# Queries of eight decode samples computed as rows, one weight place fewer and one key place more, sigmoids of the gates put off

## The chip, the cores and the metric

The kernel runs on one core of a Trainium2 chip. The metric is the time of one execution on the device, in microseconds (us). The core has a matmul engine (PE, with its weight loads shown apart as PEld), VectorE (DVE), ScalarE (ACT), GpSimd (POOL), and a queue (SP) that here only issues DMAs; 16 DMA engines move data between HBM and on-chip memory.

## The reference

One decoder layer serves a prompt of 256 tokens and 8 samples of one token each, with the same weights (float32).

```python
h = rms_norm(x, g_norm1) * (1.0 + sc1) + sh1
proj = h @ w_in
q, k, v, glu_a, glu_b, gate_a, gate_c = jnp.split(proj, ...)
q = rms_norm(q.reshape(B, S, N_HEADS, HEAD_DIM), g_q)      # 8 heads x 64
k = rms_norm(k.reshape(B, S, N_HEADS, HEAD_DIM), g_k)
attn = moba_attention(q, k_all, v_all, pos0, alibi_slopes()) @ w_attn_proj
u = glu_a * jax.nn.sigmoid(glu_b)
cv = depthwise_causal_conv(conv_in, w_dwconv) + b_dwconv    # 31 taps, 512 channels
cv = jax.nn.silu(layer_norm(cv, g_conv_ln, b_conv_ln)) @ w_conv_proj
mix = (jax.nn.sigmoid(gate_a) * attn + jax.nn.sigmoid(gate_c) * cv) @ w_out
x = x + gt1 * mix
h2 = rms_norm(x, g_norm2) * (1.0 + sc2) + sh2
x = x + gt2 * ((jax.nn.silu(f_g) * f_u) @ w_ffn_out)
```

`sh1`, `sc1`, `gt1` and the rest come from `silu(c) @ w_ada + b_ada`, with a `c` for the prompt and for each sample. In `moba_attention` every query of a sample scores 2,048 cached positions (16 pages of 128), ranks the 8 blocks of 256 by the mean score, and keeps the best three and its own position. The cached keys and values are found by a page table: 4.2 MB of keys and as much of values for each sample.

## The kernel before

The program has a stream of instructions for each engine, written by hand in the order in which they run; semaphores tie them together. Activations lie transposed: 1,024 channels as 8 tiles of 128 partitions, and 264 columns, 256 of the prompt and 8 of the samples. `fp32r` products are made from split operands: a weight tile and an activation each become a high part (ACT copies it, rounded) and a low part (the rest after subtraction), and three matmuls (high by low, low by high, high by high) add up in one bank.

**Before the loop.** PE runs tiles q0 to q3, k0 to k3, v0 to v3, a0 and b0 of `w_in`. q0 goes unsplit (`tile`, L1452, float32). Each of the others (`split`, L1465 to L1467, 24 matmuls) needs the high part of its weights from ACT (`high`, tensor `phi`, a ring of four) and the low part (`rest`, tensor `wrest`, which lies over the weights themselves). POOL makes the low parts (L589), DVE that of q2 (L1027). ACT takes each finished tile out of its bank (`raw`), squares q and k for the head norm, and PE sums the squares (`head_sums`, L1496). `spread_norm` (L1510) spreads the inverse roots, and `head_norm` on DVE (L1046) applies them.

The samples' queries are the last 8 columns of tiles q0 to q3. Once q3 is out, ACT squares them, PE sums them (L1523), ACT takes the root, DVE normalises (L1032), PE turns them into rows in 12 small matmuls (L1527, L1528) amid tile k0, ACT and DVE split them (`qsplit`), and `spread_query` (L1482) copies the query of one sample to all partitions, amid tile k1.

**Scores.** `multiply` (L1057) and `add_up` (L1064) on DVE take a quarter of one sample's keys: 4 of 16 pages, 128 x 2,048 elements each. A sample has four such quarters ("halves" by the parameter's name). Keys come by gathers that POOL issues (`gather_k`, 2.1 MB, half of a sample), into three places: two in `kring`, the third in place 2 of the weight ring `wring`. A gather waits until the chunk three before it is multiplied. Four quarters and the multiply of a fifth run before the loop.

**The loop over b = 0 to 7.** Iteration b finishes the choice of blocks and the softmax of sample b, weighs the values of sample b-1 (`weigh_values`, L1604, 16 matmuls of 512 columns that the profile counts as 32), does head b of the prompt's attention, a part of the convolution (20 taps for b < 6: ACT multiplies, POOL adds, L578), and two or three tiles of the gates (`g0` to `g15`), which ACT passes through a sigmoid as it takes them out of their bank. DVE meanwhile scores sample b+1, in four slots between its small operations. The weights of the gate tiles are `mix0` to `mix6`, loaded alternately into places 0 and 1; the third tile of a `mix` (`THIRD`) is finished in the next iteration, and only then may SP issue the load that takes its place.

**After the loop.** UNITS: 8 tiles of the convolution's projection (`cp`), 8 of attention's (`ap`), 8 of the output (`o`), 44 of the FFN's first and 8 of its second matmul. For each, ACT makes the high part (`whi`) and DVE the low part (`wlo`, L1129), in a ring of four.

**Weights.** SP issues all weight loads in the order of SLOTS, each when the former load of its place is used up. PLACE says which place: before, q, k, v and glu go to places 1, 2, 0 and 1.

## Time and profile before

| | |
|---|---|
| median of 3 runs | 591.69 us (584.13, 591.69, 594.33) |
| the profiled execution | 585.78 us, its span 584.0 us |
| granted TensorE clock, mean | 0.958 |
| PE busy | 523.6 us (90%) |
| DVE busy | 394.2 us (67%) |
| ACT busy | 292.1 us (50%), of it 46.2 us loads of activation tables |
| POOL busy | 170.0 us (29%) |
| DMA | 159.31 MB, 273 GB/s over the span |

Times below count from the start of the span. By the timeline the program has four stretches: up to 39 us the first loads and the modulation; 39 to 106 us the tiles q to b0; 106 to 300 us the loop; then the units up to 584 us. A busy share is an average over these; what bounds a stretch is read from it.

### The profile page before, as it was taken

Reading aid. Unit: us, or ns where it says so; the run is one execution under the profiler, and the core shown is the slowest. Engines: PE = TensorE matmul, PEld = TensorE weight load, DVE = VectorE, ACT = ScalarE, POOL = GpSimd, SP = SyncE. Lnnn points to the kernel's source line nnn. Section 1 sums busy time; section 2 is a strip of 40 time slices with the busy share of each in tenths; the row PEclk is TensorE's granted clock in tenths of the full one; section 3 lists DMA queues with packets and bytes.
Section 4 is the critical chain, followed back from the end, with each engine's and each line's share of the span. In section 5 each row is a group of like instructions: output and inputs, shape, how many; then the busy total and the mean of one; then the engine's idle time right before and its main releaser. Section 6 shows DMA issues by size and latency. Waiting matters only on the chain.

```text
span 584.0 us, 10410 instructions
## 1 busy us (share of the span) xinstructions
PE 523.6 (90%) x4180; PEld 441.1 (76%) x4180; DVE 394.2 (67%) x602; ACT 292.1 (50%) x519; POOL 170.0 (29%) x232
## 2 busy tenths in 40 slices
PE   3769899988979879798798999899999999999997
PEld 3658678865655646556458888799999999999996
DVE  1742674789999998999765865567565656554441
ACT  3144433587777877655653532293444444434331
POOL 8326377287778776750100000000000000000000
PEclk9589898897999999999979999999999999999999
DMA  8999459698999999999676989946466446476501
GB/s 306 370 369 388 165 189 346 224 357 296 405 399 397 420 401 416 366 366 414 260 296 245 387 291 374 364 148 213 150 221 206 147 158 164 122 192 169 153 20 38
DMA packets 82128, 159.31 MB, mean 273 GB/s; under 512 B 2573, under 2 KB 61113, under 8 KB 76952
## 3 DMA queue, kind: packets, MB, share of 16 engines
q1 hardware_dynamic: 76256, 89.27, 45.8%
q0 software_dynamic: 5120, 67.71, 28.9%
q10 hardware_dynamic: 703, 1.67, 0.8%
q8 instruction: 33, 0.54, 0.4%
q14 instruction: 16, 0.12, 0.1%
HBM read 156.39 MB, written 2.72 MB: 272 GB/s over the span
## 4 chain that ended last, share of the span: by engine, by line
PE 57%; DVE 21%; DMA 10%; issue 5%; ACT 4%; POOL 1%; SPq 1%; ACTq 1%; DVEq 0%; POOLq 0%
PE acc L1580 12%; PE acc L1581 12%; PE acc L1582 12%; DVE prod L1057 7%; DMA wring<-in_w_in 6%; DVE sall L1064 4%; PE acc L1452 3%; DMA wring<-in_w_ffn_in 2%; PE acc L1465 2%; PE acc L1467 2%; PE acc L1466 2%; DMA pr<-in_page_table 2%; PE acc L1384 2%; PE chain L1604 2%; ACT L623 1%
## 5 line engine op out<-in xcount | busy, mean ns | idle before, releaser
L1129 DVE TENSOR_TENSOR wlo<-wring,whi 128x1024 fp32r<-128x1024 f32 (+2 forms) x84 | 92.0, 1097 | 72.2 <-ACT whi L623 71.4
L623 ACT ACTIVATE whi<-wring 128x1024 fp32r<-128x1024 f32 (+2 forms) x84 | 80.1, 958 | 83.2 <-PE acc L1582 77.4
L1580 PE MATMUL acc<-xlo,whi 128*128 128x264 f32 x384 | 110.2, 287 | 3.5 <-DVE wlo L1129 1.3
L1581 PE MATMUL acc<-xhi,wlo 128*128 128x264 f32 x384 | 108.8, 283 | 0.0
L1582 PE MATMUL acc<-xhi,whi 128*128 128x264 f32 x384 | 108.8, 283 | 0.0
L578 POOL TENSOR_TENSOR cvT<-cvT,cprod 128x256 f32<-128x256 f32 x120 | 87.9, 732 | 42.4 <-ACT cprod L623 27.6
L1452 PE MATMUL acc<-hT,wring 128*128 128x264 f32 x336 | 92.1, 418 | 3.7 <-DMA wring<-in_w_in 3.3
L1580 PEld LDWEIGHTS acc<-xlo,whi 128*128 128x128 f32 x384 | 72.3, 188 | 5.8 <-issue 3.1
L1452 PEld LDWEIGHTS acc<-hT,wring 128*128 128x128 f32 x336 | 63.3, 200 | 17.6 <-DMA wring<-in_w_in 3.7
L1064 DVE TENSOR_REDUCE sall<-prod 128x32 f32<-128x2048 f32 x32 | 73.0, 2281 | 0.4
L1581 PEld LDWEIGHTS acc<-xhi,wlo 128*128 128x128 f32 x384 | 72.4, 188 | 0.1
L1582 PEld LDWEIGHTS acc<-xhi,whi 128*128 128x128 f32 x384 | 72.0, 187 | 0.0
L623 ACT ACTIVATE cprod<-u,vt 128x256 f32<-128x256 f32 x120 | 53.6, 500 | 13.7 <-POOL cvT L578 12.5
L1581 PE MATMUL acc<-fhi,wlo 128*128 128x264 f32 x208 | 59.2, 284 | 0.0
L1582 PE MATMUL acc<-fhi,whi 128*128 128x264 f32 x208 | 58.9, 283 | 0.0
L1057 DVE TENSOR_TENSOR prod<-kring,qbc 128x2048 f32<-128x2048 f32 x22 | 50.0, 2273 | 1.3 <-PE qbc L1482 0.7
L1580 PE MATMUL acc<-flo,whi 128*128 128x264 f32 x176 | 50.0, 284 | 0.3 <-ACT yn L623 0.3
L623 ACT ACT_TABLE_LOAD x36 | 46.2, 1283 | 2.3 <-PEq L1772 1.7
L589 POOL TENSOR_TENSOR wrest<-wring,phi 128x1024 fp32r<-128x1024 f32 x14 | 33.9, 2428 | 39.4 <-ACT phi L623 39.3
L1582 PEld LDWEIGHTS acc<-fhi,whi 128*128 128x128 f32 x208 | 39.1, 188 | 0.0
L1581 PEld LDWEIGHTS acc<-fhi,wlo 128*128 128x128 f32 x208 | 39.1, 188 | 0.0
L1465 PE MATMUL acc<-hsplit,phi 128*128 128x264 f32 x120 | 37.7, 314 | 0.8 <-POOL wrest L589 0.8
...
## 6 DMA issues: line engine op xcount, KB each, us to landing
...
```

Of the source, the lines that this page charges most:

```text
L578: g.tensor_tensor(cvT[:, t, 0:S], cvT[:, t, 0:S], cprod[:, i % CONV_RING, :], ALU.add)\
L589: g.tensor_tensor(low, w, high.bitcast(F32), ALU.subtract).then_inc(rest_by_pool, 1)
L623: return nc.scalar.activation(out, in_, f, **kw)
L1057: v.tensor_tensor(prod[:, :, :], k_place[chunk % K_RING][:, g:g + n, :], qbc[b % 2][:, :].unsqueeze(1).to_broadcast([P, n, A]), ALU.mult). ...
L1064: v.tensor_reduce(sall[:, b % 2, n * half:n * half + n, :].rearrange("p g h -> p (g h)"), prod[:, :, :].rearrange("p g (h d) -> p (g h) d" ...
L1129: v.tensor_tensor(wlo[:, place, 0:n, :], w, whi[:, place, 0:n, :].bitcast(F32), ALU.subtract)\
L1384: ins = mm(bank[32 * t:32 * t + 32, 0:P], cT[:, kk, :], w[:, kk, P * t:P * t + P], start=kk == 0, stop=kk == KD - 1)
L1452: ins = mm(bank[:, 0:R], w[:, k, P * t:P * t + P], src[:, k, :], start=k == 0, stop=k == KD - 1)
L1465: mm(bank[:, 0:R], high[:, k, :], hlo[:, k, :], start=k == 0, stop=False)
L1580: mm(bank[:, 0:R], whi[:, place, k - k0, :], lo[:, k, :], start=k == 0, stop=False)
L1581: mm(bank[:, 0:R], wlo[:, place, k - k0, :], hi[:, k, :], start=False, stop=False)
L1582: ins = mm(bank[:, 0:R], whi[:, place, k - k0, :], hi[:, k, :], start=False, stop=k == nk - 1)
```

## The change

1. **Queries as rows.** When the weights of q are there, 8 matmuls multiply the samples' 8 columns of `hT` by all 512 columns of q, in four row groups of one bank (`chain`, zeroed earlier by a DVE memset that moves here from the end of the head norms). ACT copies the bank, and one matmul adds the four groups up into rows 0 to 7 and 32 to 39 of `psS`. ACT squares them, DVE reduces, ACT takes the root, DVE multiplies by the gain and the inverse root, and ACT and DVE split them. `spread_query(0)` stands amid tile q1, `spread_query(1)` after k0. The old way (one sum, 12 turning matmuls, their copies) is gone.
2. **Places.** Place 2 of the ring holds only `ada2` before the keys; q, k, v, glu go to places 1, 0, 1, 0, and the `mix` loads start with place 1. So k waits for `ada3`, v for q, and glu for k.
3. **Scores earlier.** Six quarters run before the loop, and slot s of iteration b does quarter 4b+6+s instead of 4b+4+s. Slots 2 and 3 of iteration 6 are empty.
4. **Gathers.** Another order between the `rest` operations, below. `rest("q2")` moves from DVE to POOL.
5. **Gates.** ACT copies the gate tiles in the loop and applies the sigmoid later in four operations over four tiles (1,056 columns) each: around the last `values`, and at units 3 and 7.
6. **Smaller.** The head norms use three banks instead of four, in two groups of three around v3 and a0; PE waits for the probabilities of sample b-1 ahead of the block sums of b; the third tile ends before the mask matmuls.

```diff
-PLACE = dict(zip(SLOTS, [0, 1, 2, 0, 1, 2, 0, 1] + [n % 2 for n in range(B - 1)]))
-PLACE.update(conv=2, attn=1, mod4=0, mod5=0, out0=3, mod6=2, out1=4, mod7=0, mod8=2, mod9=0, mod10=3, mod11=4)
+PLACE = dict(zip(SLOTS, [0, 1, 2, 0, 1, 0, 1, 0] + [(n + 1) % 2 for n in range(B - 1)]))
+PLACE.update(conv=2, attn=0, mod4=1, mod5=1, out0=3, mod6=2, out1=4, mod7=1, mod8=2, mod9=1, mod10=3, mod11=4)
...
+            pool.dma_start(grow, g_q.rearrange("(o d) -> o d", o=1).to_broadcast([32 + B, DH])).then_inc(grow_in, 16)
...
-            for name in ON_POOL:
+            pool.wait_ge(w_full[PLACE["q"]], 32 * LOADS["q"])
+            gather_k(0)
+            pool.wait_ge(qpart_ready, 1)
+            for _, _, name in SPLITS:
                 rest(name)
-                if name == "q1":
-                    gather_k(0)
-                if name == "k0":
+                if name == "q3":
                     gather_k(1)
+                if name == "k2":
+                    pool.wait_ge(ada_used, 3)
+                    gather_k(2)
                 if name == "v0":
-                    pool.wait_ge(acc_full, NUMBER[LAST_FILL["k"]] + 1)
-                    gather_k(2)
-                if name == "v2":
                     gather_k(3)
-                if name == "v3":
+                if name == "a0":
+                    gather_k(4)
+                if name == "b0":
                     gather_v(0, 0)
                 if name == "b1":
-                    gather_k(4)
+                    gather_k(5)
...
-                gather_k(CH * b + 5)
+                gather_k(CH * b + 6)
                 add_taps(b, 2)
-                gather_k(CH * b + 6)
+                gather_k(CH * b + 7)
...
-            for t in range(KD):
+            def input_high(t):
                 act.wait_ge(h_ready, min(t + 1, H_BY_DVE))
                 if t >= H_BY_DVE:
                     act.wait_ge(h_by_act, t - H_BY_DVE + 1)
                 func(hhi[:, t, :], hT[:, t, :], ACT.Copy).then_inc(hhi_ready, 1)
+            input_high(0)
+            input_high(1)
+            act.wait_ge(consts, 3)
+            act.wait_ge(qpart_ready, 1)
+            func(pvm[:, :], chain[:, :], ACT.Copy).then_inc(qpart_copied, 1)
+            for t in range(2, 5):
+                input_high(t)
+            act.wait_ge(qrow_ready, 1)
+            func(qsq, psS[both, :], ACT.Square).then_inc(qsq_ready, 1)
+            for t in range(5, KD):
+                input_high(t)
+            act.wait_ge(qss_ready, 1)
+            func(qroot, qss, ACT.Sqrt, scale=1.0 / DH, bias=eps[both, :]).then_inc(qroot_ready, 1)
             high("q2")
+            act.wait_ge(qfull_ready, 1)
+            func(qsplit[both, :], qfull, ACT.Copy).then_inc(qs_ready, 1)
             raw("q", 0)
             high("q3")
+            func(snat, qfull[0:B, :].rearrange("p (a n) -> p a n", a=2), ACT.Copy).then_inc(qs_ready, 1)
...
             raw("q", 3)
...
             square("q", 3)
+            high("k2")
             raw("k", 0)
...
-                freed(func(gates[:, n, :], bank[:, 0:R], ACT.Sigmoid), f"g{n}")
+                freed(func(gates[:, n, :], bank[:, 0:R], ACT.Copy), f"g{n}")
+            def open_gates(first):
+                for n in range(first, first + 4):
+                    wait_freed(act, f"g{n}")
+                func(gates[:, first:first + 4, :], gates[:, first:first + 4, :], ACT.Sigmoid).then_inc(gates_open, 1)
...
+            open_gates(8)
             values(B - 1)
+            open_gates(12)
...
+                if n_unit in (3, 7):
+                    open_gates(n_unit - 3)
...
+            v.memset(chain[:, :], 0.0).then_inc(chain_zero, 1)
...
-            for t in range(KD):
+            def input_low(t):
                 dve.wait_ge(hhi_ready, t + 1)
                 v.tensor_tensor(hlo[:, t, :], hT[:, t, :], hhi[:, t, :].bitcast(F32), ALU.subtract).then_inc(hlo_ready, 1)
-            rest("q2")
+            by_head = "p (h d) -> p h d"
+            for t in range(3):
+                input_low(t)
+            dve.wait_ge(qsq_ready, 1)
+            v.tensor_reduce(qss, qsq.rearrange(by_head, d=DH), AX.X, ALU.add).then_inc(qss_ready, 1)
+            at_gain = mark(v.tensor_tensor(qgain.rearrange(by_head, d=DH), psS[both, :].rearrange(by_head, d=DH),
+                                           grow.unsqueeze(1).to_broadcast([32 + B, H, DH]), ALU.mult))
+            input_low(3)
             dve.wait_ge(qroot_ready, 1)
-            step(v.reciprocal(qroot, qroot))
-            v.scalar_tensor_tensor(qsn, qT[:, :, S:R], vec[:, V_GQ:V_GQ + 1], qroot, ALU.mult, ALU.mult).then_inc(qsn_ready, 1)
+            at_root = mark(v.reciprocal(qroot, qroot))
+            dve.wait_ge(dve_step, at_root)
+            v.tensor_tensor(qfull.rearrange(by_head, d=DH), qgain.rearrange(by_head, d=DH),
+                            qroot.unsqueeze(2).to_broadcast([32 + B, H, DH]), ALU.mult).then_inc(qfull_ready, 1)
+            for t in range(4, 6):
+                input_low(t)
             dve.wait_ge(qs_ready, 1)
-            v.tensor_tensor(qsplit[32:32 + B, :], psS[32:32 + B, :], qsplit[32:32 + B, :].bitcast(F32),
+            dve.wait_ge(qfull_ready, 1)
+            v.tensor_tensor(qsplit[32:32 + B, :], qfull[32:32 + B, :], qsplit[32:32 + B, :].bitcast(F32),
                             ALU.subtract).then_inc(qlo_ready, 1)
+            for t in range(6, KD):
+                input_low(t)
...
-            score(0, 0)
-            score(0, 1)
-            score(0, 2)
+            for half in range(STEPS):
+                score(0, half)
+            score(1, 0)
             dve.wait_ge(head_root, 1)
             v.reciprocal(headsums, headsums).then_inc(head_inv, 1)
-            score(0, 3)
-            for n in range(4):
-                head_norm(n)
-            dve.wait_ge(norm_read, 4)
-            v.memset(chain[:, :], 0.0).then_inc(chain_zero, 1)
-            multiply(1, 0)
-            for n in range(4, 6):
+            score(1, 1)
+            for n in range(6):
                 head_norm(n)
...
+                def multiply_next(slot):
+                    to, half = divmod(STEPS * b + 6 + slot, STEPS)
+                    if to < B:
+                        multiply(to, half)
...
-                if b >= 1:
-                    multiply_next(0)
+                multiply_next(0)
...
+                dve.wait_ge(gates_open, 3 + t // 4)
...
-            tile("q0", w, 0, hT)
-            split("q1")
+            pe.wait_ge(chain_zero, 1)
+            pe.wait_ge(gs1_ready, 2)
+            for k in range(KD):
+                rows = slice(32 * (k % 4), 32 * (k % 4) + B)
+                ins = mm(chain[rows, :], hT[:, k, S:R], w[:, k, :], start=k < 4, stop=k >= 4)
+            ins.then_inc(qpart_ready, 1)
+            tile("q0", w, 0, hT, k1=2)
+            pe.wait_ge(consts, 3)
+            pe.wait_ge(qpart_copied, 1)
+            mm(psS[both, :], rowsel, pvm[:, :], start=True, stop=True).then_inc(qrow_ready, 1)
+            tile("q0", w, 0, hT, k0=2)
+            split("q1", k1=4)
+            pe.wait_ge(qs_ready, 1)
+            pe.wait_ge(qlo_ready, 1)
+            spread_query(0)
+            split("q1", k0=4)
             split("q2")
             head_sums(0)
             split("q3")
             head_sums(1)
-            split("k0", k1=2)
-            pe.wait_ge(qsq_ready, 1)
-            mm(chain[:, 0:32], halves[:, :], qsq.rearrange("p t b -> p (t b)"), start=True, stop=True).then_inc(qsq_summed, 1)
-            split("k0", k0=2, k1=6)
-            pe.wait_ge(qsn_ready, 1)
-            for t in range(4):
-                nc.tensor.transpose(psS[0:B, P * t:P * t + P], qsn[:, t, :], ident[:, :])
-                ins = mm(psS[32:32 + B, P * t:P * t + P], qsn[:, t, :], ident[:, :], start=True, stop=True)
-            ins.then_inc(qs_turned, 1)
-            split("k0", k0=6)
-            split("k1", k1=3)
-            pe.wait_ge(qs_ready, 2)
-            pe.wait_ge(qlo_ready, 1)
-            spread_query(0)
-            split("k1", k0=3)
+            split("k0")
+            spread_query(1)
             head_sums(2)
+            split("k1")
             head_sums(3)
             split("k2")
             head_sums(4)
             head_sums(6)
             split("v0", k0=4)
             head_sums(7)
-            spread_query(1)
             split("v1")
             split("v2")
-            split("v3", k1=4)
-            for n in range(4):
+            for n in range(3):
                 spread_norm(n)
-            split("v3", k0=4)
-            for n in range(4, 6):
+            split("v3")
+            split("a0")
+            for n in range(3, 6):
                 spread_norm(n)
-            split("a0")
             split("b0")
...
+                if b >= 1:
+                    pe.wait_ge(p_ready, b)
...
+                if b - 1 in THIRD:
+                    tile(THIRD[b - 1], mix, 2, hT, k0=4, k1=6)
                 if b >= 1:
                     turn_values(b - 1)
                 else:
                     split("a1")
-
                 if b - 1 in THIRD:
-                    tile(THIRD[b - 1], mix, 2, hT, k0=4, k1=7)
+                    tile(THIRD[b - 1], mix, 2, hT, k0=6)
...
-                if b - 1 in THIRD:
-                    tile(THIRD[b - 1], mix, 2, hT, k0=7)
```

**On PE, the start of the q tiles** (`acc` is the bank of tile q0, then of q1; `chain` and `psS` are the banks of the queries). Before:

```order
66 L1441 MATMUL acc<-ident,prod 128x128 [waits rows_by_dve] x2
67 L1452 MATMUL acc<-hT,wring 128x264 [waits h_ready,acc_free1,w_full1]
68 L1452 MATMUL acc<-hT,wring 128x264 [waits h_ready] x4
69 L1452 MATMUL acc<-hT,wring 128x264 [waits h_by_act] x3
70 L1465 MATMUL acc<-hsplit,phi 128x264 [waits hlo_ready,acc_free0,rest_by_pool]
```

Now:

```order
66 L1479 MATMUL acc<-ident,prod 128x128 [waits rows_by_dve] x2
67 L1553 MATMUL chain<-wring,hT 8x512 [waits gs1_ready,chain_zero,w_full1]
68 L1553 MATMUL chain<-wring,hT 8x512 x7
69 L1490 MATMUL acc<-hT,wring 128x264 [waits h_ready,acc_free1]
70 L1490 MATMUL acc<-hT,wring 128x264 [waits h_ready]
71 L1558 MATMUL psS<-pvm,pg 40x512 [waits qpart_copied,consts]
72 L1490 MATMUL acc<-hT,wring 128x264 [waits h_ready] x3
73 L1490 MATMUL acc<-hT,wring 128x264 [waits h_by_act] x3
74 L1502 MATMUL acc<-hsplit,phi 128x264 [waits hlo_ready,acc_free0,rest_by_pool]
```

Nine matmuls of 512 columns stand ahead of and amid q0; the rows from L1523 to L1528 amid k0 are gone.

**On DVE, iteration 6 of the loop** (`prod` and `sall` are the multiply and the sum of a quarter; `u`, `cvT` the layer norm of the convolution). Before:

```order
262 L1218 TENSOR_TENSOR s<-s,small 128x136 [waits mb_ready]
263 L1064 TENSOR_REDUCE sall<-prod 128x32 [waits k_used]
264 L1224 TENSOR_REDUCE tiny<-s 128x8 [waits e_ready]
265 L1113 TENSOR_SCALAR cprod<-acc 128x264 [waits acc_full]
266 L1115 TENSOR_TENSOR cvT<-cvT,cprod 128x1056 [waits acc_free0]
267 L1117 TENSOR_TENSOR u<-cvT 128x4x264 [waits dve_step]
268 L1057 TENSOR_TENSOR prod<-kring,qbc 128x2048 [waits scored,k_full0]
269 L1231 TENSOR_TENSOR tiny<-small,s 128x8 [waits tot_ready]
270 L1233 RECIPROCAL tiny<-tiny 128x8 [waits dve_step]
```

Now:

```order
269 L1255 TENSOR_TENSOR s<-s,small 128x136 [waits mb_ready]
270 L1261 TENSOR_REDUCE tiny<-s 128x8 [waits e_ready]
271 L1148 TENSOR_SCALAR cprod<-acc 128x264 [waits acc_full]
272 L1150 TENSOR_TENSOR cvT<-cvT,cprod 128x1056 [waits acc_free0]
273 L1152 TENSOR_TENSOR u<-cvT 128x4x264 [waits dve_step]
274 L1268 TENSOR_TENSOR tiny<-small,s 128x8 [waits tot_ready]
275 L1270 RECIPROCAL tiny<-tiny 128x8 [waits dve_step]
```

Slots 2 and 3 are empty, so two multiplies and two sums are gone from between the small operations; the small operations stand as before.

**On POOL, between the low parts of the weights** (`wrest`). Before:

```order
52 L589 TENSOR_TENSOR wrest<-wring,phi 128x8x128 [waits w_full0,phi_ready,acc_full,rows_ready]
53 L553 DMA kring<-in_cache_k,rowof 128x4096
54 L589 TENSOR_TENSOR wrest<-wring,phi 128x8x128 [waits phi_ready] x2
55 L553 DMA kring<-in_cache_k,rowof 128x4096
56 L589 TENSOR_TENSOR wrest<-wring,phi 128x8x128 [waits phi_ready] x4
57 L553 DMA wring<-in_cache_k,rowof 128x4096 [waits acc_full]
58 L589 TENSOR_TENSOR wrest<-wring,phi 128x8x128 [waits phi_ready] x2
59 L553 DMA kring<-in_cache_k,rowof 128x4096 [waits k_used]
60 L589 TENSOR_TENSOR wrest<-wring,phi 128x8x128 [waits phi_ready]
61 L553 DMA vring<-in_cache_v,rowof 128x4096
```

Now:

```order
56 L561 DMA kring<-in_cache_k,rowof 128x4096 [waits w_full0,w_full1,acc_full,rows_ready]
57 L597 TENSOR_TENSOR wrest<-wring,phi 128x8x128 [waits phi_ready,qpart_ready]
58 L597 TENSOR_TENSOR wrest<-wring,phi 128x8x128 [waits phi_ready] x2
59 L561 DMA kring<-in_cache_k,rowof 128x4096
60 L597 TENSOR_TENSOR wrest<-wring,phi 128x8x128 [waits phi_ready] x3
61 L561 DMA wring<-in_cache_k,rowof 128x4096 [waits ada_used]
62 L597 TENSOR_TENSOR wrest<-wring,phi 128x8x128 [waits phi_ready] x2
63 L561 DMA kring<-in_cache_k,rowof 128x4096 [waits k_used]
64 L597 TENSOR_TENSOR wrest<-wring,phi 128x8x128 [waits phi_ready] x4
65 L561 DMA kring<-in_cache_k,rowof 128x4096 [waits k_used]
66 L597 TENSOR_TENSOR wrest<-wring,phi 128x8x128 [waits phi_ready]
67 L561 DMA vring<-in_cache_v,rowof 128x4096
```

The first gather stands ahead of the first low part, which waits for the queries' matmuls; six chunks of keys instead of five are gathered ahead of the loop's taps (the last ones are not among these rows), and the first values come behind the low part of b0, which needs the gated unit's weights.

## Rows read from the trace of the kernel before

**Rows 1.** windows: us, length; busy us of PE, PEld, DVE, ACT, POOL; clock, DMA share, GB/s.

```profile
39.00:44.30 5.30, 5.17 (x17) 4.09 (x17) 4.38 (x8) 4.94 (x12) 3.44 (x2) 0.68 1.05 387
44.30:47.30 3.00, 3.00 (x26) 2.97 (x25) 2.55 (x6) 1.65 (x3) 1.18 (x1) 1.00 1.06 391
63.00:67.00 4.00, 3.96 (x18) 3.23 (x19) 3.36 (x2) 1.00 (x4) 0.99 (x1) 0.64 0.61 192
152.70:177.00 24.30, 20.70 (x117) 13.41 (x116) 23.89 (x32) 18.35 (x39) 18.36 (x25) 1.00 1.03 397
252.00:283.00 31.00, 26.78 (x147) 18.28 (x145) 29.98 (x42) 17.66 (x32) 6.73 (x9) 1.00 0.94 374
```

**Rows 2.** timeline of PE: start, us, instruction, idle before and its releaser.

```profile
39.13 5.51 PE L1452 MATMUL acc<-hT,wring 128*128 128x264 f32 x16 [2.32 <-DMA wring<-in_w_in]
57.11 0.27 PE L1527 MATMUL psS<-ident,pg 128*8 128x128 f32 x1
59.18 0.40 PE L1465 MATMUL acc<-hsplit,phi 128*128 128x264 f32 x1
63.04 0.46 PE L1482 MATMUL qbc<-qsplit,qsel 40*128 40x512 f32 x1 [1.76 <-DVE qsplit L1034]
```

**Rows 3.** timeline of DVE before the loop and at its start.

```profile
40.83 4.89 DVE L1021 TENSOR_TENSOR hsplit<-hT,hsplit 128x264 fp32r<-128x264 f32 x8 [0.92 <-ACT hsplit L623]
62.21 0.68 DVE L1034 TENSOR_TENSOR qsplit<-psS,qsplit 8x512 fp32r<-8x512 f32 x1 [5.47 <-ACT qsplit L623]
63.60 2.29 DVE L1057 TENSOR_TENSOR prod<-kring,qbc 128x2048 f32<-128x2048 f32 x1 [0.71 <-PE qbc L1482]
105.97 0.16 DVE L1160 COPY gsT<-small 128x4 f32<-128x4 f32 x1 [9.40 <-PE small L1618]
```

**Rows 4.** page, costliest groups: busy us, mean ns, idle before.

```profile
L623 ACT ACT_TABLE_LOAD x36 | 46.2, 1283 | 2.3 <-PEq L1772 1.7
L589 POOL TENSOR_TENSOR wrest<-wring,phi 128x1024 fp32r<-128x1024 f32 x14 | 33.9, 2428 | 39.4 <-ACT phi L623 39.3
```

**Rows 5.** chain that ended last: start, us, what.

```profile
30.04 9.05 DMA wring<-in_w_in
...
128.95 2.29 DVE sall L1064
149.06 1.28 ACT L623
150.36 0.32 ACT s L623
...
191.09 26.40 DMA wring<-in_w_in
217.54 3.71 PE acc L1452 x8
223.99 1.28 ACT L623
229.84 2.30 DVE sall L1064
```

**Rows 6.** timeline of DVE, the sums that end two iterations.

```profile
154.93 2.29 DVE L1064 TENSOR_REDUCE sall<-prod 128x32 f32<-128x2048 f32 x1
179.41 2.29 DVE L1064 TENSOR_REDUCE sall<-prod 128x32 f32<-128x2048 f32 x1
```

**Rows 7.** timeline of PE, iteration 6 of the loop.

```profile
256.90 3.62 PE L1604 MATMUL chain<-vring,pg 128*8 128x512 f32 x32
282.71 0.39 PE L1618 MATMUL small<-quad,sall 128*128 128x4 f32 x2 [0.81 <-DVE sall L1064]
```

**Rows 8.** timeline of ACT around the last values.

```profile
295.45 2.10 ACT L623 ACTIVATE cvT<-cvT,vt 128x264 f32<-128x264 f32 x4
301.61 0.60 ACT L623 ACTIVATE pvm<-chain 128x512 f32<-128x512 f32 x1 [2.40 <-PE chain L1604]
```

**Rows 9.** timeline of DVE, low parts of attention's rows.

```profile
315.67 1.46 DVE L1268 TENSOR_TENSOR fhi<-oT,fhi 128x264 fp32r<-128x264 f32 x4 [0.49 <-ACT fhi L623]
```

74 lines of the change are left out of this document (31 added, 43 removed).

## The prediction

> **What bounds the kernel now.** I read the windows first: the busy time of each engine by stretch says which engine can end it. In an ordinary iteration of the loop DVE is busy 23.89 of 24.30 us, PE 20.70, and the DMA engines move 397 GB/s at a share of 1.03 [rows 1]. So DVE sets the pace and the DMA has next to nothing to spare; a saving on PE, ACT or POOL is worth only what DVE's idle time holds. Iteration 6 is the exception: PE 26.78 and DVE 29.98 of 31 us. Before the loop it is PE: DVE stands idle 9.40 us until PE's first block sums at 105.97 [rows 3]. The FFN at the end is PE's alone, and the change leaves it as it is. The timelines then show what lies in PE's way before the loop, and the chain of waits which waits in the loop count.
>
> **Queries as rows (before the loop, PE's path).** Out go the 12 turning matmuls, 57.11 to 59.18: 2.1 us [rows 2]; the wait for the split queries, 1.76 us [rows 2]; and perhaps the slow stretch behind that wait. In 63 to 67 us the granted clock is 0.64 [rows 1]; between the levels 2.4 and 1.2 GHz that is 2.9 us at the low one, or 1.4 us lost. Together 5.3 us. In come eight matmuls of 512 columns in four row groups. The nearest row is `weigh_values`, 16 such in 3.62 us [rows 7], so 1.8 us, and at most 3.6 at the low clock. The adding matmul uses the whole array and gets no such overlap: four times 3.62/16 is 0.9 us, 1.8 at the low clock. The stretch from 39 to 44.3 has clock 0.68 [rows 1], so I take 3.0 for both (bounds 2.7 and 5.4).
>
> Then the wait at the new `spread_query(0)`. Behind the adding matmul come in turn: ACT 0.6 [rows 8], four DVE operations of 512 columns at 0.68 [rows 3], a small reciprocal, taken as 0.35, ACT 0.6, and three low parts of `hT` that stand between, 4.89/8 = 0.61 each [rows 3]: 6.1 us. PE has six matmuls of q0 (5.51/8 = 0.69 each [rows 2], 4.1) and half of q1 (12 of 26 in 3.00 us [rows 1], 1.4) to cover it. It waits 0.6 us, and a little more for the last two low parts. I take 0.7, with bounds 0 and 4. In 3.7, out 5.3: **-1.6 us**. The bounds of the parts give -2.6 to +4.1, and up to +5.5 if the slow stretch stays all the same.
>
> **All low parts on POOL** cost POOL one more of 2.43 us [rows 4]. In the old trace POOL waits 39.3 us for ACT's high parts [rows 4], so it is ACT's order that paces it: 0. Without this cover each low part costs PE up to 2.4.
>
> **Zeroing `chain`** moves 0.4 us or so of DVE work (the price of 512 columns lies under the 0.68 of a two-input operation [rows 3]) ahead of the tiles of x. The chain then runs through the q load, 30.04 to 39.09 [rows 5], so it can cost all of it or nothing: **+0.4**.
>
> **Six quarters before the loop.** The scores can start about 13 us earlier than 63.60 [rows 3], near 50.5. The two added operations and a half, 3 x 2.28, lie in DVE's 9.40 us of idle time. The first slot's multiply now also stands ahead of iteration 0's block sums, so iteration 0 has the same DVE work behind them as before, and 1 to 5 have four full slots as before: 24.48 us from one end to the next [rows 6]. The work saved is all in iteration 6. There PE runs on from DVE's scores and waits only 0.81 us for the last sum [rows 7]; its order (two gate tiles, two sums over the convolution, the prompt's scores) does not change, and the small chain on DVE does not wait for the quarters. So of 9.1 us that leave DVE, **-0.8** arrive.
>
> **Sigmoids put off.** The program now holds 16 table loads instead of 36: 20 x 1.28 us [rows 4] leave ACT. What counts is where the chain runs through one: at 149.06 and at 223.99 [rows 5], 1.28 us each. The first lies in iteration 1, from 128.95 [rows 5] to 154.93 [rows 6], 26.0 us, which is 1.5 more than 24.48: **-1.5**. The second lies in the stretch from 179.41 [rows 6] to 229.84 [rows 5], two iterations in 50.4 instead of 49.0. In the same stretch PE waited for a load of gate weights that took 26.40 us, and then ran eight matmuls in 3.71 us instead of about 2 [rows 5]. That load is issued when the third tile is done, which now is before the mask matmuls, 1 to 2 us earlier, and it was about 1 us late. Both causes go: **-1.4**. Iteration 0 keeps its sigmoid of the gated unit and its table loads: 0.
>
> What comes back: four sigmoids of 1,056 columns. Four of 264 take 2.10 us [rows 8], the upper price of one; half is the lower. The first has 2.40 idle us of ACT before it [rows 8] for itself and a table load of 1.28, so it may end a little late; the others stand between high parts that are made three units ahead. **+0.5**, bounds 0 and 4.
>
> On the loads, the row shows 1.28 us, and the operation behind starts at once (149.06 and 1.28 is 150.34, and the exponential starts at 150.36 [rows 5]). The Trainium skill, "ScalarE: Activation LUTs", section "What ACT_TABLE_LOAD costs", adds a drain of 1.38 us for each switch. By it the two switches on the chain would give 2.8 us more. No such gap stands in the row.
>
> **Places and gathers.** k is issued when `ada3` is used, some 4 us later than before, and v and glu one block later than before. The q load took 9.05 us from issue [rows 5]. k, issued near 36 with the first gather beside it (together 4.2 MB at 387 GB/s [rows 1], 11 us behind q's end at 39), is there near 50, and ACT wants it near 52. v and glu have 10 us and more. I cost this at 0; it hides behind q1 to q3, and the margin is 2 us. In the loop each gather keeps its distance to its use: 0.
>
> **Sum.** -1.6 + 0.4 - 0.8 - 1.5 - 1.4 + 0.5 = **-4.4 us**. The profiled execution took 585.8 us, 5.9 less than the median of the three runs, which lie 10 us apart. Against it the sum gives 581.4, against the median 587.3. I cannot tell which the next runs resemble, and take the middle, 588.7 - 4.4 = **584.3 us**.
>
> **The rivals** (all from 588.7).
>
> A. *The queries' path gains nothing.* DVE's low parts of `hT` took 0.61 us each beside POOL's first low part, and those of attention's rows, of the same shape, 1.46/4 = 0.37 with POOL at rest [rows 3, 9]. POOL's low part of q2 now falls on the gain, the inverse root and the split of the queries. If it holds them up for its 2.4 us, PE waits that much longer and may pay another 1.4 at the low clock: -0.6, **588.1 us**. For it: the rows above. Against it: my prices were read beside POOL's work already. This is what the Trainium skill says in "SBUF — State Buffer", under the rule that the shared port pair is an exclusive lock: a DVE operation with two inputs there and a GpSimd operation that reads it exclude each other for a whole instruction. The trace of before agrees with it. Chance 0.17.
>
> B. *DVE, not PE, was the bound of iteration 6.* Then two quarters, 9.1 us, come off instead of 0.8: -12.7, **576.0 us**. For it: DVE is busier there (29.98 against 26.78 [rows 1]). Against it: PE's own order. Chance 0.13.
>
> C. *Weights too late, slower than before.* With two places, k, v and glu are each asked for one block later. If each lands 3 us after ACT wants it (for k, that is a landing at 55 instead of 50), PE waits 3 us each time and pays about 1.7 for the clock behind it, as 3.71 instead of 2 us shows [rows 5]: +14.1, in all +9.7, **598.4 us**. It decides from a landing of k after 52. For it: a load of 26.40 us in the full loop [rows 5]. Against it: at 63 to 67 us the DMA share was 0.61 [rows 1], so there was room. Chance 0.07.
>
> D. *The drain of the page's rule counts*: -7.2, **581.5 us**. Chance 0.05.
>
> My forecast has 0.58. The range reaches from rival B to beyond A and the base's own scatter: **575 to 593 us**. A measurement of this kernel tells about 2%, 12 us, from no change. Faster by more than that (under 580) are most of B, a part of D and a tenth of the forecast: 0.20. Slower by more (over 603) is only the worst of C: 0.03. Within: 0.77.
>
> **What the new profile would show.** Right: `spread_query(0)` near 50 us and the first multiply near 50.5; no low clock around 64; the first block sums at 103 to 105; iterations 1 to 5 at 24.4 us each; no idle time of DVE for keys; in iteration 6 PE without a gap and DVE with 5 us or more of idle time; 16 table loads. Wrong would be: PE waiting for loads of `w_in` in 50 to 90 us, a new low clock in q1, DVE idle for `kring` in the loop, iteration 6 shorter by more than 3 us, or units after the loop that wait for `gates`.

## The result, and the profile after

The changed kernel takes 590.85 us (median of 20 runs, 588.01 to 593.93), the kernel before, run beside it, 586.11 us (20 runs, 581.46 to 594.33): ratio 1.0091, 95% interval 1.007 to 1.0113. It is 5.3 us slower by the ratio. The prediction said 4.4 us faster. The measured time lies inside its range of 575 to 593 us, but the kernel moved the other way, by less than 2%. Ratios here leave out executions more than 1.5% above their kernel's fastest, which medians include (one took 1702 us; two of the profiled ones, with spans of 601.4 and 594.6 us, are among them).

The profiled execution took 590.27 us, its span 588.5 against 584.0 us; the mean granted clock fell from 0.958 to 0.945. To see where the 4.5 us of the spans arise, I took one DVE instruction that stands once in each iteration, the last product of own probabilities (`gs<-s,tiny`), and the copy of the first block sums in front of the loop. Times in us from the start of the span:

| | before | after | later by |
|---|---|---|---|
| tile q1 taken out by ACT | 47.59 | 55.69 | 8.1 |
| tile k2 taken out by ACT | 71.21 | 74.62 | 3.4 |
| first block sums | 105.97 | 107.28 | 1.3 |
| iteration 0 done | 128.22 | 133.71 | 5.5 |
| iteration 1 done | 154.18 | 158.97 | 4.8 |
| iteration 2 done | 178.67 | 185.68 | 7.0 |
| iteration 4 done | 229.10 | 234.80 | 5.7 |
| iteration 5 done | 253.51 | 258.71 | 5.2 |
| iteration 7 done | 295.62 | 300.18 | 4.6 |
| end | 584.0 | 588.5 | 4.5 |

So three places matter: the tiles of q, iteration 0 (4.2 us), and iteration 2 (2.2 us, of which iteration 4 gives 1.6 back). Between q1 and the loop most of the delay is made up again. Windows of the new trace (length; busy us of PE, PEld, DVE, ACT, POOL; clock, DMA share, GB/s), to be read against [rows 1]:

```profile
44.30:48.00 3.70, 3.70 (x17) 2.70 (x16) 2.59 (x6) 2.67 (x6) 0.23 (x1) 1.00 0.99 416
48.00:54.00 6.00, 2.70 (x18) 2.07 (x17) 5.94 (x6) 2.68 (x5) 5.85 (x3) 1.00 0.03 12
54.00:58.00 4.00, 3.88 (x19) 3.88 (x20) 3.97 (x4) 1.65 (x3) 1.82 (x2) 0.57 0.57 176
107.30:133.70 26.40, 20.50 (x115) 16.34 (x114) 20.04 (x31) 16.82 (x37) 12.86 (x18) 0.94 1.03 371
159.00:185.70 26.70, 24.16 (x123) 16.50 (x122) 24.36 (x32) 16.36 (x38) 18.41 (x25) 0.87 1.01 391
258.70:284.00 25.30, 23.52 (x129) 16.63 (x128) 19.93 (x34) 6.54 (x19) 5.44 (x7) 0.93 0.91 356
```

From 48 to 54 us PE is busy 2.70 of 6 us, DVE and POOL all the time, and the DMA engines move 12 GB/s: nobody had asked them for anything. In iteration 0 DVE, which sets the pace elsewhere, idles 6.4 of 26.4 us.

**The tiles of q.** The timeline of DVE, then of POOL (start, us, instruction, idle before and its releaser), which answer to [rows 3]:

```profile
48.02 0.76 DVE L1053 TENSOR_TENSOR hsplit<-hT,hsplit 128x264 fp32r<-128x264 f32 x2
48.81 2.74 DVE L1072 TENSOR_TENSOR qsplit<-oT,qsplit 8x512 fp32r<-8x512 f32 x1
51.58 2.83 DVE L1053 TENSOR_TENSOR hsplit<-hT,hsplit 128x264 fp32r<-128x264 f32 x2
54.33 2.27 DVE L1097 TENSOR_TENSOR prod<-kring,qbc 128x2048 f32<-128x2048 f32 x1
```

```profile
47.77 6.00 POOL L597 TENSOR_TENSOR wrest<-wring,phi 128x1024 fp32r<-128x1024 f32 x2 [3.49 <-ACT phi L634]
53.93 0.99 POOL L561 DMA_INDIRECT kring<-in_cache_k,rowof  x1 [0.15 <-issue]
```

The subtraction of the queries' low row takes 2.74 us where the same shape took 0.68 [rows 3], and the two low parts of `hT` behind it 2.83, where the pair at 48.02 took 0.76. Beside them POOL makes two low parts back to back, 3.0 us each instead of 2.43 [rows 4]. DVE is held twice, some 2.06 us each time. (Once more, off PE's path: one low part of `hT` at 42.88 takes 1.70 us beside POOL's low part of 41.93 to 44.28; alone, at 46.85, it takes 0.41.) The first multiply starts at 54.33: nine microseconds earlier than before, and four later than predicted. PE waited for both operations of DVE, and then ran at the low clock, 0.57 in 54 to 58 us (timeline of PE):

```profile
51.70 0.46 PE L1519 MATMUL qbc<-qsplit,qsel 40*128 40x512 f32 x1 [2.39 <-DVE qsplit L1072]
54.12 0.43 PE L1502 MATMUL acc<-hsplit,phi 128*128 128x264 f32 x1 [1.03 <-DVE hsplit L1053]
```

**Iteration 0.** The chain of waits (start, us, what) goes through a load of mixing weights:

```profile
95.83 0.37 SPq L453
96.20 0.04 issue
96.24 25.88 DMA wring<-in_w_in
122.12 0.04 issue
122.17 3.50 PE acc L1490 x8
```

The timeline of PE says the same: 4.34 us of waiting, then eight matmuls in 3.50 us, where the next eight take 2.05. And the timeline of POOL shows what else the DMA engines were given meanwhile:

```profile
122.17 3.50 PE L1490 MATMUL acc<-hT,wring 128*128 128x264 f32 x8 [4.34 <-DMA wring<-in_w_in]
125.60 0.57 PE L1699 MATMUL small<-tiny,ones 8*128 8x8 f32 x2
126.10 2.05 PE L1490 MATMUL acc<-hT,wring 128*128 128x264 f32 x8
```

```profile
95.07 0.96 POOL L561 DMA_INDIRECT kring<-in_cache_k,rowof  x1 [0.16 <-issue]
...
98.61 0.96 POOL L561 DMA_INDIRECT vring<-in_cache_v,rowof  x1 [0.16 <-issue]
...
104.47 0.95 POOL L561 DMA_INDIRECT wring<-in_cache_k,rowof  x1 [0.16 <-issue]
```

These are chunk 4, the first values of sample 0, and chunk 5. In the kernel before, whose load of the first mixing weights was issued at 95.0, only one gather, at 101.31, stood in the 20 us behind it. In 92 to 96 us, just ahead of them, the DMA engines of the changed kernel moved nothing.

DVE, too, waited for a gather before the loop, for chunk 2 (timeline of DVE):

```profile
77.20 2.29 DVE L1097 TENSOR_TENSOR prod<-wring,qbc 128x2048 f32<-128x2048 f32 x1 [4.13 <-DMA wring<-in_cache_k,rowof]
```

**Iteration 2.** No load is late, but PE idles in front of the transpose of the largest products and in front of the next small product, and the second eight matmuls run at half clock, 3.89 us (timeline of PE):

```profile
172.46 0.27 PE L1693 MATMUL small<-ident,tiny 128*8 128x128 f32 x1 [2.06 <-DVE tiny L1239]
172.57 2.65 PE L1490 MATMUL acc<-hT,wring 128*128 128x264 f32 x8
175.71 0.59 PE L1699 MATMUL small<-tiny,ones 8*128 8x8 f32 x2 [0.48 <-DVE tiny L1248]
176.23 3.89 PE L1490 MATMUL acc<-hT,wring 128*128 128x264 f32 x8
```

**What came as predicted.** 16 table loads, in place of the 36 of [rows 4] (groups of ACT: busy us, mean ns, idle before), and ACT's exponential at 129.88 right behind a load that began at 128.59:

```profile
L634 ACT ACT_TABLE_LOAD x16 | 20.5, 1283 | 2.0 <-PEq L1807 1.7
...
128.59 1.28 ACT L634 ACT_TABLE_LOAD   x1
129.88 0.32 ACT L634 ACTIVATE s<-s 128x136 f32<-128x136 f32 x1
```

Iterations 6 and 7 together take 41.5 us (from 258.71 to 300.18) instead of 42.1, with DVE idle 5.4 us of iteration 6, and PE's last block sums do not wait:

```profile
287.27 0.39 PE L1654 MATMUL small<-quad,sall 128*128 128x4 f32 x2
```

### The profile page after: what moved, and what is told of

Read it like the earlier page. It is cut to its first block, busy times and chain, and to the rows that moved or that the text cites. A ratio compares the mean times of both kernels' runs of the same rounds, so it can differ in the third digit from the quotient of the medians.

```text
span 588.5 us, 10443 instructions
## 1 busy us (share of the span) xinstructions
PE 527.2 (90%) x4184; PEld 445.3 (76%) x4184; DVE 397.1 (67%) x604; ACT 272.4 (46%) x503; POOL 173.7 (30%) x237
## 4 chain that ended last, share of the span: by engine, by line
PE 57%; DVE 22%; DMA 11%; issue 5%; ACT 2%; POOL 2%; SPq 0%; DVEq 0%; POOLq 0%; ACTq 0%
PE acc L1614 12%; PE acc L1615 12%; PE acc L1616 12%; DVE prod L1097 8%; DMA wring<-in_w_in 6%; PE acc L1490 6%; DVE sall L1104 4%; DMA cprod<-in_state_conv 2%; DMA wring<-in_w_ffn_in 2%; PE acc L1502 2%; PE acc L1422 2%; PE acc L1504 2%; PE acc L1503 2%; PE chain L1638 1%; PE small L1533 1%
## 5 line engine op out<-in xcount | busy, mean ns | idle before, releaser
L1490 PE MATMUL acc<-hT,wring 128*128 128x264 f32 x336 | 99.2, 441 | 4.3 <-DMA wring<-in_w_in 4.3
L1490 PEld LDWEIGHTS acc<-hT,wring 128*128 128x128 f32 x336 | 67.5, 213 | 22.2 <-issue 6.7
L634 ACT ACTIVATE cprod<-u,vt 128x256 f32<-128x256 f32 x120 | 55.3, 502 | 21.7 <-POOL cvT L586 20.5
L597 POOL TENSOR_TENSOR wrest<-wring,phi 128x1024 fp32r<-128x1024 f32 x15 | 37.0, 2474 | 20.4 <-ACT phi L634 19.7
L1502 PE MATMUL acc<-hsplit,phi 128*128 128x264 f32 x120 | 36.6, 305 | 1.9 <-DVE hsplit L1053 1.0
L1504 PE MATMUL acc<-hsplit,phi 128*128 128x264 f32 x120 | 34.7, 290 | 0.0
## 6 DMA issues: line engine op xcount, KB each, us to landing
wring<-in_w_in SPq DMA_DIRECT2D x4, 768.0 KB, 21.4
```

The costliest lines, as they stand in the source:

```text
L597: g.tensor_tensor(low, w, high.bitcast(F32), ALU.subtract).then_inc(rest_by_pool, 1)
L634: return nc.scalar.activation(out, in_, f, **kw)
L1490: ins = mm(bank[:, 0:R], w[:, k, P * t:P * t + P], src[:, k, :], start=k == 0, stop=k == KD - 1)
L1502: mm(bank[:, 0:R], high[:, k, :], hlo[:, k, :], start=k == 0, stop=False)
L1504: ins = mm(bank[:, 0:R], high[:, k, :], hhi[:, k, :], start=False, stop=k == KD - 1)
```

## The experiments

The theory: the gathers, issued where the low parts' order puts them, crowd the load of mixing weights and cost some 4 us; POOL's low parts beside the queries' rows cost about 1.5; the third tile, moved ahead, brings the low clock of iteration 2; the sigmoids gain what was predicted. An edit's worth is the difference of two ratios times 586 us. Each such difference is uncertain by 2 to 2.7 us, so a worth below that is not told from zero. The profiles are single executions. Kernels with the same instructions up to the loop began it at 107.28, 107.62 and 110.47 us (the change, sigmoids in the loop, third tile where it was), so a few microseconds between two profiles prove little by themselves.

**Low part of q2 held on POOL.**

```diff
             for _, _, name in SPLITS:
+                if name == "q2":
+                    pool.wait_ge(qlo_ready, 1)
+                    pool.wait_ge(hlo_ready, KD)
                 rest(name)
```

> The changed kernel, but GpSimd makes the low part of q2 only when DVE has made the queries' low row and all eight low parts of hT. Theory (GpSimd and DVE hold each other up while the queries' rows are made): the split of the queries on DVE takes 0.7 us instead of 2.74, the last low parts of hT 0.6 instead of 2.83, the first multiply stands near 50.5 us instead of 54.3, q1 ends near 52 instead of 55.7; later tiles win less, since ACT and GpSimd pace them: the first block sums some 1 us earlier, the end 0.5 to 1.5 us earlier than the changed kernel, ratio to the kernel before 1.007. Rival (the late rows were what cost the whole 5 us): ratio 1.000. Rival (the holding moves the wait to PE, for q2 and q3): no change or slower, 1.009 to 1.012.

Ratio 1.0062 (1.0026 to 1.0098), 1.7 us less than the change, which by itself is not told from nothing. DVE's timeline:

```profile
50.31 0.68 DVE L1075 TENSOR_TENSOR qsplit<-oT,qsplit 8x512 fp32r<-8x512 f32 x1
51.02 0.78 DVE L1056 TENSOR_TENSOR hsplit<-hT,hsplit 128x264 fp32r<-128x264 f32 x2
52.12 2.29 DVE L1100 TENSOR_TENSOR prod<-kring,qbc 128x2048 f32<-128x2048 f32 x1 [0.32 <-issue]
```

Both operations are back at 0.68 and 0.78 us: that POOL held them up is shown. q1 ends at 53.30, k0 to k3 exactly 2.0 us earlier each. But 2 us earlier, the load of v was late (timeline of ACT), and the loop started at 108.34, no earlier:

```profile
74.72 1.06 ACT L637 ACTIVATE phi<-wring 128x1024 fp32r<-128x1024 f32 x1 [1.71 <-DMA wring<-in_w_in]
```

This is rival C's mechanism, on a small scale and for v alone, which the slower tiles of q hid in the change.

**Gathers earlier.**

```diff
-                if name == "q3":
+                if name == "q1":
                     gather_k(1)
-                if name == "k2":
+                if name == "q3":
                     pool.wait_ge(ada_used, 3)
                     gather_k(2)
-                if name == "v0":
+                if name == "k2":
                     gather_k(3)
-                if name == "a0":
+                if name == "v0":
                     gather_k(4)
-                if name == "b0":
+                if name == "v2":
                     gather_v(0, 0)
-                if name == "b1":
+                if name == "a0":
                     gather_k(5)
```

> The changed kernel, but with the key gathers issued earlier: chunk 1 behind the low part of q1, chunk 2 behind q3, chunk 3 behind k2, chunk 4 behind v0, the values of sample 0 behind v2, chunk 5 behind a0. Theory (the gathers crowd the load of mix0 from 95 us on, and PE waits 4.3 us for it in iteration 0 at 122 and runs at the low clock behind it): the load of mix0 takes under 18 us instead of 25.9, PE does not wait for it, DVE does not wait 4.1 us for chunk 2 before the loop, iteration 0 ends 3 to 4 us earlier, and so does the kernel: ratio 1.001 to 1.003. Rival (the wait for mix0 covers one that comes anyway, DVE's four slots): no wait for mix0, but the first iteration ends within 1 us of where it did, ratio 1.008 to 1.010.

Ratio 1.0017 (0.999 to 1.0044): 4.3 us less than the change. The load is issued in two parts, of 1,024 and 512 KB. From issue to landing they take (least, median, most of the two; the change first, then this kernel):

```profile
DMA to landing us min/median/max: 24.1/25.0/25.9
DMA to landing us min/median/max: 9.1/9.7/10.3
```

PE does not wait (timeline), and iteration 0 takes 21.4 us (109.38 to 130.77) at a DMA share of 0.63 (window):

```profile
119.76 1.94 PE L1490 MATMUL acc<-hT,wring 128*128 128x264 f32 x8
121.64 0.38 PE L1699 MATMUL small<-tiny,ones 8*128 8x8 f32 x2
```

```profile
109.40:130.80 21.40, 18.20 (x113) 15.01 (x111) 19.57 (x32) 16.38 (x36) 12.24 (x17) 1.00 0.63 222
```

The loop starts 2.1 us later than in the change, where the clock was 1.00 while v3 ran and here 0.70 (92 to 96 us), and iteration 0 still ends 2.9 us earlier.

**Chunks 1 and 2 alone earlier**, the rest as in the change.

```diff
-                if name == "q3":
+                if name == "q1":
                     gather_k(1)
-                if name == "k2":
+                if name == "q3":
                     pool.wait_ge(ada_used, 3)
                     gather_k(2)
```

> The changed kernel, but with chunks 1 and 2 of the keys alone gathered earlier (behind q1 and q3); chunks 3, 4, 5 and the values of sample 0 stay behind v0, a0, b1 and b0. Theory (what costs are the gathers beside mix0 from 95 us on, not DVE's wait of 4.1 us for chunk 2 before the loop, where DVE has idle time): no wait for chunk 2, but mix0 still takes some 26 us and PE waits 4 us for it: ratio 1.007 to 1.010. Rival (DVE's late scores before the loop were the cost): ratio 1.002 to 1.004.

Ratio 1.0105 (1.0077 to 1.0134). DVE no longer waits for chunk 2, and nothing is won. The load of mixing weights still takes up to 23.9 us and PE waits, though less than 4 us, since here the loop began 2.8 us later (timeline):

```profile
122.98 2.05 PE L1490 MATMUL acc<-hT,wring 128*128 128x264 f32 x8 [2.32 <-DMA wring<-in_w_in]
```

Against the kernel with all gathers earlier this one is 5.2 us slower (uncertain by 2.3). So it is the later gathers, those beside the weights, that cost. The profiles of all runs agree: where those gathers stay late (five with a landing time) the two parts of the first mixing weights take 19.9 to 26.3 us, and where they go early (five) 9.1 to 14.0.

**Third tile where it was.**

```diff
-                if b - 1 in THIRD:
-                    tile(THIRD[b - 1], mix, 2, hT, k0=4, k1=6)
                 if b >= 1:
                     turn_values(b - 1)
...
                 if b - 1 in THIRD:
-                    tile(THIRD[b - 1], mix, 2, hT, k0=6)
+                    tile(THIRD[b - 1], mix, 2, hT, k0=4, k1=7)
...
                 ins.then_inc(mask_ready, 1)
+                if b - 1 in THIRD:
+                    tile(THIRD[b - 1], mix, 2, hT, k0=7)
```

> The changed kernel, but the third tile of each mixing block stands again where it stood before: three of its matmuls behind the turned values, the last behind the mask. Theory (with it moved ahead PE has nothing to do while ACT and DVE work on the mask, idles 2.06 us, and the matmuls behind that run at the low clock): iteration 2 takes 24.5 to 25 us instead of 26.7, the clock of iterations 1 to 5 is above 0.9 instead of 0.87, the end is 1 to 2 us earlier, ratio 1.006. Rival (the order does not matter, DVE sets the pace): ratio 1.009, the iterations as they are. Rival (the early issue of the gates' weights was worth something): slower, 1.011 or more.

Ratio 1.0101 (1.0065 to 1.0136): nothing gained, where the theory had 1.006. Its profiled execution (span 601.4 us) cannot show what iteration 2 gained, and shows another thing, in the chain and in a window of iteration 2:

```profile
147.77 38.52 DMA wring<-in_w_in
```

```profile
180.00:185.00 5.00, 0.00 (x0) 0.00 (x0) 0.00 (x0) 0.00 (x0) 0.00 (x0) 0.50 1.01 420
```

A load of weights took 38.52 us with the DMA engines full, and for 5 us every engine stood still behind it. The next load's issue on SP, at 170.44, itself took 12.08 us; in the changed kernel's loop no such issue took more than 2.15. The third tile's new place alone does not bring the low clock, for with it and the gathers earlier iteration 2 took 24.7 us; what brought it in the change stays open.

**Sigmoids in the loop again.**

```diff
-                freed(func(gates[:, n, :], bank[:, 0:R], ACT.Copy), f"g{n}")
+                freed(func(gates[:, n, :], bank[:, 0:R], ACT.Sigmoid), f"g{n}")
```

and without `open_gates` and the waits for it.

> The changed kernel, but the gates' sigmoids are taken in the loop again, as the tiles come (36 table loads). Theory (the prediction's term for them stands: 1.5 in iteration 1 and a part of 1.4 in iterations 2 to 3, against 0.5 for the four late sigmoids): 1.5 to 2.5 us slower than the changed kernel, ratio 1.012 to 1.013, with table loads on the chain of waits in the loop. Rival (putting them off is what cost the 5 us, in the loop's end and the units behind it): faster than the changed kernel, ratio 1.000 to 1.003. Rival (table loads are off DVE's path altogether): ratio 1.009.

Ratio 1.0139 (1.01 to 1.0179): 2.8 us slower than the change, just clear of its uncertainty of 2.6. Putting them off gains in the changed kernel; the prediction had 2.4.

**Kernel before with the sigmoids put off, twice.** The edit is the reverse of the last, made in the kernel before, with the four `open_gates` where the change has them.

> The kernel before with one part of the change alone: the gates' sigmoids put off (copies in the loop, four wide sigmoids at its end and among the units), 16 table loads instead of 36. Theory (this part was worth what undoing it showed, 0.0139 - 0.0091 of 586 us, or 2.8 us; the prediction had 1.5 + 1.4 - 0.5 = 2.4): 1.5 to 3 us faster than before, ratio 0.995 to 0.998, iteration 1 of the loop near 24.5 us instead of 26.0. Rival (its gain came only where the changed kernel's loop was disturbed anyway): ratio 0.999 to 1.001.

> The kernel before with the gates' sigmoids put off, once more, since the first measurement's interval (0.9975 to 1.0066) holds both cases. Theory (worth 2 to 3 us): ratio 0.995 to 0.998. Rival (worth nothing where PE waits for late weights in the same iterations): 0.999 to 1.002; in its profile iteration 1 is shorter than 26.0 us and a later one longer than before.

Ratios 1.0021 (0.9975 to 1.0066) and 1.007 (1.0036 to 1.0104). My theory of 2 to 3 us gained falls here: alone, this part brings nothing or costs some us. The windows of iterations 1 and 2 in the second kernel, and its wait (timeline of PE):

```profile
128.29:153.62 25.33, 22.29 (x118) 14.69 (x117) 25.07 (x31) 14.84 (x39) 19.90 (x27) 0.93 0.91 360
153.62:180.57 26.95, 24.22 (x119) 15.69 (x120) 24.14 (x31) 15.99 (x37) 17.93 (x24) 0.87 1.03 408
```

```profile
167.87 3.89 PE L1465 MATMUL acc<-hT,wring 128*128 128x264 f32 x8 [0.57 <-DMA wring<-in_w_in]
```

Iteration 1 gains 0.6 us, iteration 2 loses 2.5, and iteration 4, in which the kernel before waited for its late weights, gains 1.4 (24.8 us instead of 26.2). The late load has moved from iteration 4 to iteration 2, where the weights, 0.57 us late, are followed by matmuls at half the clock. In the profile of the first such kernel (span 594.6 us) that wait is 15.02 us, behind a load of 40.21 us, and SP's next issue took 12.30 us. That the edit does not gain is measured. Two profiles do not show how often a load comes late with and without it, so the reason stays open.

**Four quarters ahead instead of six.**

```diff
-            score(1, 0)
...
-            score(1, 1)
...
-                    to, half = divmod(STEPS * b + 6 + slot, STEPS)
+                    to, half = divmod(STEPS * b + 4 + slot, STEPS)
...
-                if name == "b1":
-                    gather_k(5)
...
-                gather_k(CH * b + 6)
+                gather_k(CH * b + 5)
```

> The changed kernel, but with the scores four quarters ahead instead of six (the two quarters of sample 1 are scored in iteration 0 again), and chunk 5 not gathered before the loop. Theory (six quarters ahead bring 0.8 us in iteration 6 and cost a gather that crowds mix0): the load of mix0 takes near 20 us instead of 25.9, PE's wait of 4.3 us for it is 0 to 1, the first iterations end 3 us earlier, iterations 6 and 7 together 1 us later: ratio 1.004 to 1.006. Rival B (DVE is the bound at the loop's end): 4 us or more are lost there, ratio 1.010 or more.

Ratio 1.0073 (1.0032 to 1.0114), 1.1 us less than the change, which is not told apart from nothing; the theory's 1.004 to 1.006 lies in the interval as well. In its profile PE does not wait for the weights, and iterations 6 and 7 take 42.0 us, as before (42.1), against 41.5 in the change. But the profiled execution (586.9 us) is the fastest of its twelve, which reach to 599.9 us, so the missing wait is not shown for the others. Rival B's loss of 4 us or more at the loop's end does not appear.

**Both repairs.** Beside the held low part, the earlier gathers, with one difference:

```diff
-                if name == "v2":
+                if name == "v3":
                     gather_v(0, 0)
```

> The changed kernel with both repairs: GpSimd's low part of q2 held until the queries' rows are done, and the key gathers earlier (chunk 1 behind q1, 2 behind q3, 3 behind k2, 4 behind v0, the values behind v3, 5 behind a0). Theory (late gathers cost 4 to 4.5 us, GpSimd beside the queries' rows 2 us at k0 and 1.3 at the loop's start, and the load of v, which was 1.7 us late with the first repair alone, is in time when the gathers have gone before it): the repairs add up, 5 to 7 us faster than the changed kernel, ratio 0.997 to 1.001; tile k0 ends near 65, the first block sums at 105 to 107, no wait for a load of w_in. Rival (they overlap, both end at the same bound, the granted clock around v3): ratio 1.001 to 1.003, the first block sums at 108 or later.

Ratio 0.9969 (0.9937 to 1.0001), 583.44 us against 586.69: 7.1 us less than the change (1.7 and 4.3 alone), and about as fast as the kernel before or 2 us faster. The repairs add up, within the uncertainty of 2.3 us. On top of the earlier gathers, holding the low part is worth 2.8 us (uncertain by 2.5, and one gather of values has moved as well). In this profile v is in time (k0 to k3 at 61.90 to 73.28 us, without a wait for w_in); that the earlier gathers see to it is not shown, for in a kernel with the same instructions up to the loop (the third tile below) v was 3.15 us late and the loop began at 107.90. The first block sums stand at 103.81. Iteration 0 takes 21.4 us, iteration 1 24.8, but iteration 2 27.9 (window of 150 to 178 us, and PE's wait in it):

```profile
150.00:178.00 28.00, 24.13 (x123) 16.17 (x122) 24.55 (x32) 16.36 (x38) 18.52 (x25) 0.88 1.02 409
```

```profile
165.54 3.89 PE L1493 MATMUL acc<-hT,wring 128*128 128x264 f32 x8 [1.65 <-DMA wring<-in_w_in]
```

So against the kernel before, 2.2 us won at the loop's start and 3.0 by the end of iteration 0 are down to 0.4 by the end of iteration 7 (295.22 against 295.62). In the loop the DMA engines are full, as the window's share of 1.02 says, and a late load takes back what was won.

**Three variants of it**: the old place of the third tile, the sigmoids in the loop, and the second gather of values issued behind the next taps.

> The kernel with both repairs, and the third tile of each mixing block where it stood before the change (three matmuls behind the turned values, one behind the mask). Theory (PE's idle 2 us in front of the transpose of the largest products brings the low clock behind it, and the block's eight matmuls in 3.9 us instead of 2.05): iteration 2, 27.9 us with both repairs, takes 25 to 26, ratio 0.991 to 0.995. Rival (the low clock and the long iteration come from the late load of weights, and that from the DMA queues, which are full): iteration 2 or another still takes 26 us or more, ratio 0.996 to 0.999.

> The kernel with both repairs, and the gates' sigmoids in the loop again. Theory (putting them off is worth 2 to 3 us wherever the loop is not held up otherwise): ratio 1.000 to 1.003. Rival (in a loop whose DMA queues are full the table loads lie beside other waits, as the kernel before with this part alone, 1.0021, suggests): ratio 0.995 to 0.998, as with both repairs.

```diff
                 else:
-                    for c in range(CH):
-                        gather_v(b, c)
+                    gather_v(b, 0)
                 add_taps(b, 1)
+                if b >= 1:
+                    gather_v(b, 1)
```

> The kernel with both repairs, and in iterations 1 to 7 the second gather of values issued behind the next group of taps, some 6 us later, so that the load of mixing weights, asked for in the same microsecond, shares the queues with one transfer less. Theory (the queues are full in the loop, and what is asked for first lands late; PE's waits of 1.65 and 0.87 us for weights go, with the low clock behind them): iteration 2 takes 25 to 26 us instead of 27.9, ratio 0.991 to 0.995. Rival (the queues are full, so the same bytes end at the same time, and the wait moves to the values): PE or DVE waits for vring or kring, ratio 0.997 to 1.001.

Ratios 0.9978 (0.9941 to 1.0014), 1.0022 (0.9995 to 1.0048) and 0.9998 (0.9973 to 1.0024). The third tile again does not matter for the time: iteration 2 takes 24.9 us instead of 27.9, as the theory had it, but iteration 4 still takes 26.4, with weights 1.28 us late, as the rival had it. Putting the sigmoids off is worth 3.1 us here (uncertain by 2.4). Later values don't help: PE still waits 1.71 us for weights in iteration 4, and now 0.50 for values:

```profile
215.90 3.89 PE L1494 MATMUL acc<-hT,wring 128*128 128x264 f32 x8 [1.71 <-DMA wring<-in_w_in]
298.05 1.90 PE L1642 MATMUL chain<-vring,pg 128*8 128x512 f32 x16 [0.50 <-DMA vring<-in_cache_v,rowof]
```

## Why the prediction was wrong

**"Places and gathers: I cost this at 0."** This step failed, and it is the largest. I followed k, v and glu to their use and found them in time, and in the change PE waited for none of them (ACT waited 0.61 us for glu). I did not follow the load after them, the first mixing weights, nor ask which gathers now stand beside it. The margin of "each gather keeps its distance to its use" was the wrong question: a gather that is in time for itself can make the load beside it late. Measured: a load of 25.9 us, a wait of 4.34 us, iteration 0 longer by 4.2 us (22.25 to 26.43), and 4.3 us back when the gathers go earlier (uncertain by 2.0). The room was there: three idle stretches of the DMA engines before the loop (12 GB/s in 48 to 54 us, 20 in 76 to 80, none in 92 to 96).

**"Queries as rows: -1.6."** The sign failed in the profiles: tile k2 came 3.4 us later. Rival A named the cause, POOL's low part over DVE's row operations, at 2.4 us once; it held DVE twice, 2.06 us each, and PE paid low clock behind it. Against rival A I had set that my prices were read beside POOL's work already. They were, but the 0.68 us of [rows 3] belongs to a subtraction with one input in PSUM, the matmul's banks (`psS`), and the new one has both in SBUF (`oT`, `qsplit`): a price is read only for the memories that its row names. The Trainium skill, "SBUF — State Buffer", section "Who interferes with whom", says that a DVE instruction with two inputs in SBUF contends with a GpSimd instruction that reads SBUF. The trace agrees: 2.74 us beside POOL's low part and, with POOL held back, 0.68. Without it, k2 still ends 1.4 us later than before (72.62 against 71.21), where the prediction had it 1.6 earlier. So the parts were mis-sized as well: q0 was taken out 4.0 us later (48.66 against 44.69), where I took 3.0 for the new matmuls, which took 2.41 (1.90 to 3.60 in the other profiles) and 1.17; and with the low part held, POOL's next one starts only at 51.93. At the loop's start 1.3 us of the delay was left. One reason is the granted clock, 1.00 in 92 to 96 us, where it was 0.64 before. That was luck of this execution: in the kernel with the third tile moved back, the same up to there, it was 0.86 and then 0.71 (96 to 100 us), and the loop began at 110.47.

**"Sigmoids put off: -1.5, -1.4, +0.5."** The sum, 2.4, was right in the changed kernel (2.8, and 3.1 with the repairs), and no unit behind the loop waited. Rival D, a drain behind each load, would have given 2.8 more, and no drain shows in the row at 128.59. But that is in part luck, since the second term's working was wrong: late weights did not go, they moved to other iterations, and in the kernel before, the same edit gained nothing.

**"Six quarters: -0.8."** Right by the profiles: 0.6 us in iterations 6 and 7, DVE idle 5.4 us of iteration 6, PE waiting in it but once (1.78 us for the largest products). Of the eight profiles with six quarters and late sigmoids, seven have 40.6 to 41.5 us for the two iterations and one 42.5 (both repairs, third tile where it was); the four profiles with four quarters have 42.0 to 42.1. No ratio tells this gain from zero. Rival B falls. Its price was the extra gather of chunk 5, which belongs to the first step.

**"Zeroing `chain`: +0.4"** and the low parts on POOL at 0: PE's first matmul on q moved from 39.13 to 39.42 us, which is less than the profiles with this start differ among themselves (38.85 to 39.88). POOL's idle time before its low parts fell from 39.4 to 20.4 us, but PE waited for them 0.87 us in all, as before (0.8). What POOL's order cost came through DVE.

Taken apart step by step, the 5.3 us are +7.1 for the late gathers and the held DVE together (4.3 and 1.7 apart), -3.1 for the sigmoids, and a rest of +1.3. The rest is the ratio of the kernel with both repairs and the sigmoids in the loop, 1.0022 (0.9995 to 1.0048), or -0.3 to 2.8 us: the queries' rows, the quarters and all else that changed. It is not told from zero, and it shuts out the -2.0 that the prediction had for rows, zeroing and quarters. The base was off as well: 588.7 us were taken, and 20 runs gave 586.11. Open is why in some executions one load of weights takes 38 to 40 us in iteration 2.
